# Local attention: TensorE turns the weights of block n-1 ahead of the projection unit of body n

## What is computed

```python
def sink_softmax(s, mask, sink):
    s = jnp.where(mask, s, -jnp.inf)
    m = jnp.maximum(jnp.max(s, axis=-1, keepdims=True), sink)
    p = jnp.exp(s - m)
    return p / (jnp.sum(p, axis=-1, keepdims=True) + jnp.exp(sink - m))

def swa_banded(q, k, v, sinks):
    B, T = q.shape[:2]
    NB = T // WINDOW
    qb = q.reshape(B, NB, WINDOW, SWA_KV_HEADS, SWA_GROUP, SWA_HEAD_DIM)
    ...
    kk = jnp.concatenate([jnp.pad(kb, shift)[:, :-1], kb], axis=2)
    vv = jnp.concatenate([jnp.pad(vb, shift)[:, :-1], vb], axis=2)
    s = jnp.einsum('bnqhgd,bnkhd->bnhgqk', qb, kk, preferred_element_type=jnp.float32) * SWA_HEAD_DIM ** -0.5
    ...
    p = sink_softmax(s, mask, sink)
    o = jnp.einsum('bnhgqk,bnkhd->bnqhgd', p.astype(v.dtype), vv)
    return o.reshape(B, T, SWA_WIDTH)
```

## Time and profile before

| | us |
|---|---|
| three runs: median (lowest to highest) | 2534.78 (2534.32 to 2543.17) |
| the profiled execution: its time | 2533.13 |
| its span, first to last instruction | 2531.4 |
| PE busy in the span | 2231.0 (88%) |
| DVE, ACT, POOL busy in the span | 1536.2 (61%), 1141.4 (45%), 368.9 (15%) |
| mean granted clock of TensorE | 0.929 of 2.4 GHz |

### The profile page before, as it was taken

How to read it: one execution, slowest core, us unless ns; L and a number is a source line. 1 busy time by engine, 2 the same in 40 slices (tenths; PEclk the granted TensorE clock), 3 DMA queues, 4 the chain that set the end, 5 groups by cost and what they waited for, 6 DMA issues and landing times. The chain is left out here.

```text
span 2531.4 us, 35779 instructions
## 1 busy us (share of the span) xinstructions
PE 2231.0 (88%) x13120; PEld 1940.8 (77%) x13121; DVE 1536.2 (61%) x2042; ACT 1141.4 (45%) x1614; POOL 368.9 (15%) x391
## 2 busy tenths in 40 slices
PE   4689999999998689899789999969669999999990
PEld 2388888888988476788589999958558888888870
DVE  2355665665665423366644545446568989899885
ACT  3233344343244220344443334333247777777874
POOL 1002211220220212222300000020011111111103
PEclk8799999999999785899989999989779999999995
DMA  8510221121120223700155555553379999999966
GB/s 342 186 43 23 67 61 43 36 70 38 33 70 19 59 52 90 241 18 4 39 168 146 150 145 148 152 186 117 116 265 390 408 402 405 405 400 408 403 245 237
DMA packets 310883, 432.17 MB, mean 171 GB/s; under 512 B 57698, under 2 KB 251730, under 8 KB 290755
## 3 DMA queue, kind: packets, MB, share of 16 engines
q1 hardware_dynamic: 289788, 369.53, 42.0%
q0 software_dynamic: 11296, 39.46, 4.2%
q10 hardware_dynamic: 9720, 22.11, 2.2%
HBM read 375.98 MB, written 57.10 MB: 171 GB/s over the span
## 5 line engine op out<-in xcount | busy, mean ns | idle before, releaser
L2646 DVE TENSOR_TENSOR ex_w_r<-ex_w,ex_wh 128x2048 fp32r<-128x2048 f32 x198 | 447.1, 2286 | 61.7 <-ACT ex_wh L2588 61.5
L2588 ACT ACTIVATE ex_wh<-ex_w 128x2048 fp32r<-128x2048 f32 x198 | 379.1, 1917 | 120.3 <-PE ex_up L2543 41.4
L2016 DVE TENSOR_TENSOR mg_w_r<-mg_w,mg_wh 128x1024 fp32r<-128x1024 f32 x94 | 115.0, 1225 | 132.5 <-ACT mg_wh L1978 132.5
L1978 ACT ACTIVATE mg_wh<-mg_w 128x1024 fp32r<-128x1024 f32 x94 | 99.5, 1059 | 174.9 <-DVE mg_out L2041 91.8
L895 PE MATMUL gd_ps<-hh,gd_wh 128*128 128x352 f32 x368 | 122.8, 334 | 10.7 <-ACT preS L615 10.7
L1965 PE MATMUL mg_psum<-hh,mg_wh 128*128 128x352 f32 x384 | 125.2, 326 | 1.7 <-PEq L1729 1.7
L1965 PE MATMUL mg_psum<-hh,mg_w_r 128*128 128x352 f32 x384 | 124.7, 325 | 0.0
L1965 PE MATMUL mg_psum<-hT_r,mg_wh 128*128 128x352 f32 x384 | 124.3, 324 | 0.0
L1965 PE MATMUL mg_psum<-mg_xh,mg_wh 128*128 128x352 f32 x384 | 124.0, 323 | 0.0
L1965 PE MATMUL mg_psum<-mg_xh,mg_w_r 128*128 128x352 f32 x384 | 123.6, 322 | 0.0
L895 PE MATMUL gd_ps<-hh,gd_w_r 128*128 128x352 f32 x368 | 118.2, 321 | 0.0
(11 more groups left out here) (636 smaller groups left out, 5981.1 us busy)
## 6 DMA issues: line engine op xcount, KB each, us to landing
ex_w<-in_w_gate_dram SPq DMA_DIRECT2D x66, 1024.0 KB, 7.9
ex_w<-in_w_up_dram SPq DMA_DIRECT2D x66, 1024.0 KB, 7.5
ex_w<-in_w_down_dram SPq DMA_DIRECT2D x66, 1024.0 KB, 8.5
ada_w<-in_w_ada_dram SPq DMA_DIRECT2D x24, 1024.0 KB, 15.7
mg_w<-in_w_in_dram SPq DMA_DIRECT2D x48, 512.0 KB, 3.7
expert_out_scratch<-ex_y ACTq DMA_DIRECT2D x33, 512.0 KB, 7.7
gd_w<-in_w_in_dram SPq DMA_DIRECT2D x32, 512.0 KB, 4.6
mg_w<-in_w_br_gdn_dram SPq DMA_DIRECT2D x24, 512.0 KB, 3.7
```

The lines of the kernel that those rows point to most:

```text
L1978: nc.scalar.activation(wh[q][:], wl[q][:], ACT.Copy).then_inc(w_high, 1)
L2016: nc.vector.tensor_tensor(wl_r[q][:], wl[q][:], wh[q][:].bitcast(F32), ALU.subtract).then_inc(w_low, 1)
L2588: nc.scalar.activation(wh[at][:], wl[b][u][:], ACT.Copy).then_inc(w_high, 1)
L2646: nc.vector.tensor_tensor(wl_r[b][u][:], wl[b][u][:], wh[at][:].bitcast(F32), ALU.subtract).then_inc(w_low, 1)
```

## The change

PE's list changes, nothing else: the turn of block n-1 is issued behind the scores of block n+1 and ahead of the projection unit of body n.

```diff
                 for n in range(NBLOCKS + 2):
                     if n + 1 < NBLOCKS:
                         scores(n + 1)
+                    if 1 <= n <= NBLOCKS:
+                        turn(n - 1)
                     if n < NBLOCKS:
                         for unit in plan[n]:
                             project(unit)
-                    if 1 <= n <= NBLOCKS:
-                        turn(n - 1)
                     if n >= 2:
                         values(n - 2)
```

## The result

| | before | changed |
|---|---|---|
| median, us (lowest to highest, six runs each) | 2534.55 (2531.40 to 2543.17) | 2557.17 (2555.69 to 2570.51) |
| ratio to before, 95% interval | | 1.0093 [1.0073, 1.0113] |
| the profiled execution: its time, us | 2533.13 | 2568.22 |
| its span, us | 2531.4 | 2566.5 |
| local-attention stage, first score matmuls to the next stage's first PE matmul, us | 214.28 | 238.97 |

The account below looks back on a forecast made before the run. PE was taken to bound the loop's middle, so its new waits add up: 3.9 + 3.9 + 6.5 + 1.35 + 4.0 + 3.4 = 23.05 us on 2534.78, some 2558 us, range 2549 to 2568.

Parts of the forecast that it names:

- head, P(2) behind T(1): Stage's head: body 2's projection, formerly done before block 1's turn, now comes behind it; 3.9 us.
- 17 plain bodies: Bodies whose early turn waits only for DVE's copy of the previous turn: 0.23 us each, 3.9 us.
- T(5), T(13), waits: Turns of blocks 5 and 13, after query-weight splits, wait for POOL's block: 3.27 us each, 6.5 together.
- T(9): Turn of block 9, after the key-weight split, waits for POOL's block: 1.35 us.
- T(21), T(25): Turns of blocks 21 and 25, after bodies without a projection, wait 2.0 us each for POOL: 4.0 together.
- clock behind T(5), T(13): One half-rate stretch of 3.3 us after each of these two turns' waits, some 1.7 us each: 3.4 us.
- tail behind V(25): Stage's end, after block 25's values: same order and waits as before, only starting later; nothing added.
- PE sets the pace, and its waits are lost: Loop's middle: PE busy 20.00 of 20 us, so every microsecond it idles there is lost.
- the joints: New transitions turn to projection and projection to values: taken as 0, up to 0.1 us each, bound 2.4 us.
- Rival 2: Weight splits stay hidden: turns of blocks 5, 9 and 13 find their block ready; 2547 us, chance 0.05.
- Rival 1: Clock falls at every long wait: six stretches, 10.2 us instead of 3.4, giving 2565 to 2568 us; chance 0.12.
- Nothing behind the stage changes: Next stage starts behind a barrier of all engines and only shifts with this one; nothing added.

Follow-up runs that it names:

- e1: Kernel before, with the turn moved ahead of the projection only in the 17 plain bodies, not in the seven that would wait for POOL; 2541.05 us, ratio 1.0009.
- e2: Kernel before, with the turn moved ahead of the projection only in bodies 1, 2, 6, 10, 14, 22 and 26; 2556.74 us, ratio 1.0077.
- e7: Changed kernel, with DVE copying the turn out before the values of the block before; 2557.19 us, ratio 1.0075 to the kernel before.
- e3: Changed kernel, with DVE's low half of each weight split moved behind the next body's reciprocal; 2549.96 us, ratio 1.0056 to the kernel before.
- e6: Changed kernel run once more without an edit, for a second trace; 2555.40 us in one run.
- e8: Kernel before, PE's order kept, with DVE's low half behind the next body's reciprocal and its turn copy before its value copy; 2528.90 us, ratio 0.9978.
- e4: Changed kernel, with 18 extra matmuls of unused result ahead of the waiting turn in bodies 6 and 14; 2554.80 us, ratio 1.0067 to the kernel before.

## Why the prediction was right

The sum was made of terms for single bodies, so each can be laid beside what the body's values started later than before, counted from S(0):

| term | forecast | measured |
|---|---|---|
| head, P(2) behind T(1) | 3.9 | 3.81 |
| 17 plain bodies | 3.9 (0.23 each) | 2.66 (0.10 to 0.20, mean 0.157) |
| T(5), T(13), waits | 6.5 | 6.19 (3.11, 3.08) |
| T(9) | 1.35 | 1.30 |
| T(21), T(25) | 4.0 | 3.99 |
| clock behind T(5), T(13) | 3.4 | 4.28 (1.61, 2.67) |
| sum, S(0) to V(25) | 23.05 | 22.26 |
| tail behind V(25) | 0 | 2.44 (0.86 in the second pair of traces) |

- *PE sets the pace, and its waits are lost.* Right. e1 and e2 put 0.15 us a body on the plain order and all the rest on the seven waits, and DVE's waits for values grew.
- *The plain body.* The wait was foreseen to the row, 0.16 us and 1.29 from scores to turn, but 0.23 us a body was too much: the joints, which the forecast set at nothing, gave 0.05 to 0.08 back (4.84 us for 4.89). That is inside the bound of 0.1 a joint. e7 shows the cause of the wait.
- *The weight splits.* Right in place, size and cause: 3.11 and 3.08 for 3.27, 1.30 for 1.35, and e3 takes them away by moving the low half alone. Rival 2 (hidden anyway) falls with that. The 0.56 us that the forecast put down to ACT's copies within these waits no run separates.
- *Bodies after one without a projection.* 1.99 and 1.99 for 2.0. No run took these two waits away, nor the one before T(0), so their causes are read from the rows and not tested.
- *The head.* The sum is right, the division of the waits was not. T(0) waited 5.62 us for the 5.7 forecast, T(1) only 0.98 for 3.0: the clock fell behind T(0), P(1) and S(3) ran slowly, and their length took the place of idle time. The forecast had said that such a fall is taken up there, and then named 3.0 us all the same; this is 2.0 of the some 5 us by which PE's waits for POOL, 22.0 us in 9, stayed below the forecast's 27 in 11. Another 2.0 are in the tail, where two waits for POOL became shorter ones for DVE: 4.0 us in 2 for 6.0 in 4.
- *The clock.* The right two waits in the profiled execution, by luck in part: the stretch behind T(13) lasted twice as long as priced, and a second trace has T(21) in T(13)'s place. Rival 1 (a fall at every wait of 2 us and more) is refused by T(25), which never fell in the six traces that have its wait, while T(0) and T(5), unfilled, fell each time. The rule of the Trainium skill beside that rival ("TensorE: Matmul & The Clock Gate", section "HAM oscillation — how this bites in real kernels") is told there of waits longer than T(25)'s 2.0 us. T(0) and T(5) agree with it; T(13) in e6, 3.07 us without a fall, does not, and T(25) does not bear on it, nor do the shorter idles that the forecast set against it.
- *The tail.* Wrong, and small: set at nothing because its order and its waits are as before, it took 2.44 us more in the first pair of traces. The forecast looked for falls only behind waits that the change makes or moves, and T(27)'s old wait of 2.0 us was followed by one in every trace with moved turns. So the stage was 24.7 us longer, where its end was forecast 20 to 23 us later; in the second pair it was 20.6.
- *Nothing behind the stage changes.* Not to be seen in one pair of traces: the first pair has 8.9 us more behind it, the second has fewer. The medians are 22.6 us apart and the stage 24.7 and 20.6 longer in the two pairs of traces, so the sum of 23.05 lies between the two, and that it comes within half a microsecond of the medians is luck.

## What to carry to other kernels

Where one engine fills a loop, a step that waits for another engine belongs behind the longest piece of its work that needs nothing from outside; price a move by asking, for each body and not for the typical one, when its input is ready and what stands before it: five bodies and the head made 19.6 of the 22.26 us. If the waits are to go instead of being hidden, look at the order on the engine that feeds the chain: a step of 2.3 us (1.2 at T(9)) that stood ahead of a reciprocal, with its own wait, cost 1.3 to 3.1 us at each of four turns, and moving it shortened the stage in both orders of PE. An idle of 3 us on TensorE may cost half as much again through the clock, so a sum for it needs both a wait and a fall, also at waits that the change leaves alone, and a second trace to tell which falls come back.

## What was not expected of the hardware

The granted clock behind a wait of the same length differs from one execution to the next, and from one turn to another. The number of traces in which a stretch at 0.50 follows the wait, of the traces that have the wait:

| wait of PE, what it stands before | us | falls |
|---|---|---|
| T(0), early order | 5.6 | 6 of 6 |
| T(5), early order | 2.9 to 3.3 | 4 of 4 |
| T(13), early order | 2.9 to 3.3 | 3 of 4 |
| T(1), old order | 2.8 | 2 of 3 |
| T(21), early order | 2.0 to 2.2 | 2 of 6 |
| T(25), early order | 2.0 to 2.2 | 0 of 6 |
| T(27), any turn early (e1 too) | 2.0 to 2.2 | 7 of 7 |
| T(27), old order (e8 too) | 2.0 to 2.2 | 0 of 3 |

The 2.78 us wait without a fall in the earlier trace rows, on which the forecast leaned against rival 1, was thus the rarer case. Behind T(1), T(5), T(13) and T(21) a fall cost 1.6 us where a stretch of some 3.3 us followed, and 2.7 in the one case where 6.7 us did. Matmuls in place of the idle time kept the clock at 1.00 at both places tried (e4). The tail, whose waits are 1 to 2 us long but many, ran at 1.00 in two traces only, the first of before and e8; what decides there, T(27) included, was not tried.
